# Reordering VectorE's work at stage changes, in the delta rule's output chain and in the last normalisation

## What is computed

```python
for l in range(DEPTH):                      # 2
    mod = (silu(c) @ w_ada[l] + b_ada[l])   # 9 vectors of 1024: shift, scale, gate for 3 sub-layers
    y = swiglu(x * (1 + scale) + shift, ffn_w_up[l, 0], ffn_w_down[l, 0])
    x = layer_norm(ALPHA * x + 0.5 * (1 + gate) * y, ln_g[l, 0], ln_b[l, 0])
    y = mixer(x * (1 + scale) + shift, w_in[l], ..., w_branch[l], w_o[l])
    x = layer_norm(ALPHA * x + (1 + gate) * y, ln_g[l, 1], ln_b[l, 1])
    y = swiglu(..., ffn_w_up[l, 1], ffn_w_down[l, 1])
    x = layer_norm(ALPHA * x + 0.5 * (1 + gate) * y, ln_g[l, 2], ln_b[l, 2])
```

## Time and profile before

| | |
|---|---|
| median of 3 runs | 1361.91 us (1359.81 to 1363.42) |
| the profiled execution, its own time | 1363.72 us |
| its span | 1362.0 us |
| mean granted TensorE clock | 0.98 of full speed |
| TensorE busy | 96% of the span |
| VectorE busy | 73% |
| ScalarE busy | 49% |
| GpSimd busy | 9% |
| DMA | 295.24 MB, mean 217 GB/s |

### The profile page before, as it was taken

How to read it: one execution, slowest core, us unless ns; L and a number is a source line. 1 busy time by engine, 2 the same in 40 slices (tenths; PEclk the granted TensorE clock), 3 DMA queues, 4 the chain that set the end, 5 groups by cost and what they waited for, 6 DMA issues and landing times.

```text
span 1362.0 us, 18522 instructions
## 1 busy us (share of the span) xinstructions
PE 1301.0 (96%) x7277; PEld 1077.8 (79%) x7277; DVE 996.4 (73%) x1294; ACT 664.4 (49%) x998; POOL 122.4 (9%) x219
## 2 busy tenths in 40 slices
PE   4799999999999999999999999999999999999996
PEld 3588887898888767888878888788888877788885
DVE  4778875597776787888667888559777669776545
ACT  2344444666744545445354444366675354544431
POOL 4101001000000011000100000100000001100000
PEclk9799999999899999999999999999989999999998
DMA  9679883866465447888659888467655543785550
GB/s 326 233 237 307 283 283 105 282 210 211 143 202 178 154 143 250 276 279 277 237 162 303 278 278 289 145 220 240 207 179 190 177 152 103 258 288 187 185 185 31
DMA packets 198342, 295.24 MB, mean 217 GB/s; under 512 B 14408, under 2 KB 162416, under 8 KB 198256
## 3 DMA queue, kind: packets, MB, share of 16 engines
q1 hardware_dynamic: 177744, 220.58, 48.7%
q0 software_dynamic: 20512, 73.48, 16.4%
HBM read 292.97 MB, written 1.05 MB: 216 GB/s over the span
## 4 chain that ended last, share of the span: by engine, by line
PE 78%; DVE 12%; ACT 4%; issue 3%; DMA 2%; POOL 1%; SPq 0%; DVEq 0%; POOLq 0%; ACTq 0%
PE pg L979 68%; DVE wlo L1620 3%; PE pt L1004 1%; DVE acc L1559 1%; ACT whi L567 1%; DMA wraw<-in_w_in_dram 1%; PE pt L959 1%; PE pt L1341 1%; PE pt L1328 1%; PE pt L1180 1%; DVE cv L1806 1%; PE pt L1343 1%; DVE gates L2068 1%; DVE acc L1644 1%; DVE x L1743 1%
## 5 line engine op out<-in xcount | busy, mean ns | idle before, releaser
L1620 DVE TENSOR_TENSOR wlo<-wraw,whi 128x1024 fp32r<-128x1024 f32 (+1 forms) x408 | 480.1, 1201 | 169.1 <-ACT whi L567 168.4
L567 ACT ACTIVATE whi<-wraw 128x1024 fp32r<-128x1024 f32 (+1 forms) x408 | 405.7, 1035 | 169.5 <-PE pg L979 106.1
L979 PE MATMUL pg<-whi,hhi 128*128 128x512 f32 x1024 | 417.2, 407 | 15.5 <-DVE wlo L1620 12.6
L979 PE MATMUL pg<-wlo,hhi 128*128 128x512 f32 x1024 | 405.8, 396 | 0.0
L979 PE MATMUL pg<-whi,hlo 128*128 128x512 f32 x1024 | 405.8, 396 | 0.0
L979 PEld LDWEIGHTS pg<-whi,hhi 128*128 128x128 f32 x1024 | 196.6, 192 | 62.6 <-DVE wlo L1620 16.1
L979 PEld LDWEIGHTS pg<-whi,hlo 128*128 128x128 f32 x1024 | 196.1, 192 | 42.8
L979 PEld LDWEIGHTS pg<-wlo,hhi 128*128 128x128 f32 x1024 | 196.7, 192 | 38.7 <-issue 0.5
L1644 DVE SCALAR_TENSOR_TENSOR acc<-aw,sc,acc 128x1024 f32<-128x1024 f32 x128 | 163.8, 1279 | 0.5 <-DMA aw<-in_w_ada_dram 0.4
L979 PE MATMUL pg<-whi,athi 128*128 128x512 f32 x352 | 138.4, 393 | 0.0
L444 POOL DMA_DIRECT2D aw<-in_w_ada_dram x128 | 67.9, 530 | 771.0 <-DVE acc L1644 736.3
(11 more groups left out here) (336 smaller groups left out, 1324.7 us busy)
## 6 DMA issues: line engine op xcount, KB each, us to landing
wraw<-in_ffn_w_up_dram SPq DMA_DIRECT2D x176, 512.0 KB, 5.5
aw<-in_w_ada_dram POOLq DMA_DIRECT2D x128, 512.0 KB, 4.4
wraw<-in_w_in_dram SPq DMA_DIRECT2D x104, 512.0 KB, 4.7
wraw<-in_ffn_w_down_dram SPq DMA_DIRECT2D x88, 512.0 KB, 4.7
pro<-in_w_ada_dram SPq DMA_DIRECT2D x16, 512.0 KB, 9.9
wraw<-in_w_branch_dram SPq DMA_DIRECT2D x16, 512.0 KB, 4.3
wraw<-in_w_o_dram SPq DMA_DIRECT2D x16, 512.0 KB, 3.7
lnw<-in_ln_g_dram POOLq DMA_DIRECT2D x5, 512.0 KB, 5.9
```

The costliest lines, as they stand in the source:

```text
L567: act.activation(hi_view(n)[:, 0:size], wraw[:, q, o:o + size], ACT.Copy).then_inc(S["w_hi"], 1)
L979: ins = pe.matmul(out_ap, a[i], b[j], start=first and n == 0, stop=last and n == 2, skip_group_check=group)
L1620: dve.tensor_tensor(lo, a, hi_view(n)[:, 0:size].bitcast(F32), ALU.subtract).then_inc(S["w_lo"], 1)
```

## The change

- Last normalisation: `normed` and `affine` of the last stage become `last_norm(t)`, four operations on halves of 512 columns: (x - mean) * gain for both halves, which needs no power, then * rstd + bias for both. Each half of a tile is stored by a DMA of its own (256 KB), four in all in place of two.
- Stage changes: `h_low` is called by quarter. The third quarter of tile 0 stays ahead of `residual(1, 1)`, the fourth goes behind `moments(1)`. At s = 1 VectorE's splits of the next stage's halves 2 and 3 go ahead of `residual(1, 0)` (they stood ahead of `residual(1, 1)` and behind `moments(1)`), and ScalarE makes all four splits before it modulates tile 0.
- Output chain: the multiplication behind GpSimd's power becomes `o_scale(t)`, called later than `o_mean(t)`; `o_raw` and `o_scale(0)` go ahead of `gated(1, 1)`; `o_mean(1)` and `o_gate(0)` go ahead of slot 57's split, `o_scale(1)` and `o_gate(1)` stay behind it.
- `column_parts` of the shift goes from slot 61 to slot 45; that of the scale stays at slot 64.

```diff
--- before.py
+++ after.py
@@ -376,9 +376,11 @@
             for t in range(NT):
-                sp.wait_ge(S["x_affine"], NT * (STAGES - 1) + t + 1)
-                sp.dma_start(out[0, t * P:(t + 1) * P, :], x[:, t, :]).then_inc(S["out"], 16)
-            sp.wait_ge(S["out"], 16 * NT)
+                for n in (0, 1):
+                    c = slice(n * 512, (n + 1) * 512)
+                    sp.wait_ge(S["x_affine"], NT * (STAGES - 1) + 2 * t + n + 1)
+                    sp.dma_start(out[0, t * P:(t + 1) * P, c], x[:, t, c]).then_inc(S["out"], 16)
+            sp.wait_ge(S["out"], 2 * 16 * NT)
 
@@ -624,13 +626,10 @@
                     h = 2 * u_next + (0 if s == 1 else 2)
-                    split(h)
-                    split(h + 1)
+                    for n in range(4 if s == 1 else 2):
+                        split(h + n)
                     modulate(at, s, 0, 0)
                     modulate(at, s, 0, 1)
-                    if s == 1:
-                        split(h + 2)
-                        split(h + 3)
                     modulate(at, s, 1, 0)
@@ -1600,14 +1599,13 @@
 
-            def h_low(at, k, t, half):
-
-                for quarter in (2 * half, 2 * half + 1):
-                    c = slice(2 * quarter, 2 * quarter + 2)
-                    dve.wait_ge(S["h_hi"], at("h_hi", 4 * (NT * k + t) + quarter + 1))
-                    dve.tensor_tensor(hlo[:, c, t * P:(t + 1) * P],
-                                      lnw[:, t, quarter * 256:(quarter + 1) * 256].rearrange("p (k s) -> p k s", k=2),
-                                      hhi[:, c, t * P:(t + 1) * P].bitcast(F32), ALU.subtract).then_inc(S["h_lo"], 1)
+            def h_low(at, k, t, quarter):
+
+                c = slice(2 * quarter, 2 * quarter + 2)
+                dve.wait_ge(S["h_hi"], at("h_hi", 4 * (NT * k + t) + quarter + 1))
+                dve.tensor_tensor(hlo[:, c, t * P:(t + 1) * P],
+                                  lnw[:, t, quarter * 256:(quarter + 1) * 256].rearrange("p (k s) -> p k s", k=2),
+                                  hhi[:, c, t * P:(t + 1) * P].bitcast(F32), ALU.subtract).then_inc(S["h_lo"], 1)
 
@@ -1653,9 +1651,9 @@
 
-                def shift(stage, t, rows=lnw):
+                def shift(stage, t):
                     dve.wait_ge(S["x_gain"], NT * stage + t + 1)
-                    dve.tensor_tensor(x[:, t, :], x[:, t, :], rows[:, 1, :], ALU.add).then_inc(S["x_affine"], 1)
+                    dve.tensor_tensor(x[:, t, :], x[:, t, :], lnw[:, 1, :], ALU.add).then_inc(S["x_affine"], 1)
 
@@ -1758,40 +1756,47 @@
 
-                    def affine(t):
+                    def last_norm(t):
 
                         dve.wait_ge(S["ln_rows"], 32 * STAGES)
-                        dve.wait_ge(S["ln_x"], at("ln_x", 2 * (NT * s + t) + 2))
-                        dve.tensor_tensor(x[:, t, :], x[:, t, :], last_rows[:, 0, :], ALU.mult).then_inc(S["x_gain"], 1)
-                        shift(STAGES - 1, t, last_rows)
+                        dve.wait_ge(S["ln_mv"], at("ln_mv", NT * s + t + 1))
+                        for n in (0, 1):
+                            c = slice(n * 512, (n + 1) * 512)
+                            dve.scalar_tensor_tensor(out=x[:, t, c], in0=x[:, t, c], scalar=mv[:, t, 0:1], in1=last_rows[:, 0, c],
+                                                     op0=ALU.subtract, op1=ALU.mult).then_inc(S["x_gain"], 1)
+                        dve.wait_ge(S["ln_rstd"], at("ln_rstd", NT * s + t + 1))
+                        for n in (0, 1):
+                            c = slice(n * 512, (n + 1) * 512)
+                            dve.wait_ge(S["x_gain"], NT * (STAGES - 1) + 2 * t + n + 1)
+                            dve.scalar_tensor_tensor(out=x[:, t, c], in0=x[:, t, c], scalar=rstd[:, t:t + 1], in1=last_rows[:, 1, c],
+                                                     op0=ALU.mult, op1=ALU.add).then_inc(S["x_affine"], 1)
 
...
                     moments(0)
-                    normed(0)
                     if 3 * l + s == STAGES - 1:
-                        affine(0)
+                        last_norm(0)
                         residual(1, 0)
...
                         moments(1)
-                        normed(1)
-                        affine(1)
+                        last_norm(1)
                         return
+                    normed(0)
                     h = 2 * u_next + (0 if s == 1 else 2)
-                    split(h)
-                    split(h + 1)
+                    for n in range(3 if s == 1 else 2):
+                        split(h + n)
                     h_low(at, s, 0, 0)
+                    if s == 1:
+                        split(h + 3)
+                    h_low(at, s, 0, 1)
                     residual(1, 0)
-                    h_low(at, s, 0, 1)
-                    if s == 1:
-                        split(h + 2)
+                    h_low(at, s, 0, 2)
                     residual(1, 1)
                     moments(1)
-                    if s == 1:
-                        split(h + 3)
+                    h_low(at, s, 0, 3)
                     normed(1)
-                    h_low(at, s, 1, 0)
-                    h_low(at, s, 1, 1)
+                    for quarter in range(4):
+                        h_low(at, s, 1, quarter)
 
@@ -2019,6 +2024,9 @@
                     dve.tensor_scalar(oss[:, c], oss[:, c], RMS_EPS, None, ALU.add).then_inc(S["o_ms"], 1)
+
+                def o_scale(t):
+                    c = slice(4 * t, 4 * t + 4)
                     dve.wait_ge(S["o_pw"], at("o_pw", t + 1))
@@ -2089,14 +2097,19 @@
                             gated(0, q - 49)
-                        if q in (55, 56):
-                            gated(1, q - 55)
+                        if q == 55:
+                            gated(1, 0)
                         if q == 52:
...
                             o_raw()
+                            o_scale(0)
+                            gated(1, 1)
+                        if q == 57:
+                            o_mean(1)
+                            o_gate(0)
                         if q == 59:
@@ -2139,8 +2152,7 @@
                         if q == 57:
-                            o_mean(1)
-                            o_gate(0)
+                            o_scale(1)
                             o_gate(1)
@@ -2154,8 +2166,8 @@
                             merged_lo(1)
-                        if q in (61, 64):
-                            column_parts(3 * l + 2, (61, 64).index(q))
+                        if q in (45, 64):
+                            column_parts(3 * l + 2, (45, 64).index(q))
                         if q == SLOTS - 4:
...
```

## The result

| | before | after |
|---|---|---|
| median of the runs taken side by side | 1362.66 us (4 runs) | 1349.8 us (1348.2 to 1352.61, 4 runs) |
| the profiled execution's own time | 1363.72 us | 1349.19 us |
| its span | 1362.0 us | 1347.5 us |
| mean granted clock | 0.980 | 0.984 |

The ratio is 0.9903 with a 95% interval of 0.9887 to 0.992: 12.9 us between the medians, faster by 1.0%. The forecast was 1349.6, in a range of 1343.5 to 1355.

The account below looks back on a forecast made before the run. TensorE was taken as the bound, so gains come only from its idle or half-clock moments and the end. 5.8 + 4.8 - 1.6 + 0.9 + 2.4 = 12.3 us took the median from 1361.9 to 1349.6, range 1343.5 to 1355.

Parts of the forecast that it names:

- Term 1: Output chain: TensorE's waits for gated output products go in both layers, with one half-clock stretch; gain 5.8 us.
- Term 2: Shift columns at slot 45: the sum fits VectorE's wait for ScalarE, merged_lo(0) comes earlier; gain 4.8 us.
- Term 3: Mixer to feed-forward: ScalarE stands for a weight unit's DMA before modulating tile 0, x comes later; loss 1.6 us.
- Term 4: Other three stage changes: one h_low quarter leaves VectorE's queue ahead of residual(1, 1); gain 0.9 us.
- Term 5: The end: halved last normalisation runs partly beside GpSimd's power, and smaller stores land sooner; gain 2.4 us.
- A: Mixer to feed-forward: the weight unit is there in time, ScalarE isn't held; 1344 to 1345 us, chance 0.12.
- B: Idle pieces at mixer to feed-forward bring half clock, or output chain keeps part of its wait; 1353 to 1354, chance 0.18.
- C: TensorE is limited elsewhere in the mixer and takes back output-chain and shift-column gains; 1358 to 1361 us, chance 0.07.
- D: Slower: each us the weight unit lands late moves x by a us in both layers; 1366 and more, chance 0.03.

Follow-up runs that it names:

- The undivided operation: Changed kernel with the gain operation of the last normalisation over a tile's 1024 columns at once in place of two halves; 1348.6 us, single run.
- the two experiments on the splits: Changed kernel with the mixer to feed-forward splits put back on both engines, 1346.46 us; with only VectorE's put back, ScalarE's new order kept, 1352.56 us.
- the four that were run in repeat: Changed kernel with one edit put back each: output chain 1357.59 us, shift columns 1353.2, last normalisation 1351.82, splits at mixer to feed-forward 1346.46.

## Why the prediction was right

The mechanisms of four terms came out as forecast and that of the fifth in part. That the median hit 1349.8 for 1349.6 is luck beyond that. By the landmarks the change's own work is -6.6 (output chain), -4.8, +1.4, -0.7 and -2.8, together 13.5 us; forecast were 12.3, and the medians gave 12.9. The forecast was also taken from a median of 1361.91, and the one beside the changed kernel was 1362.66. Each of these is smaller than the 4 us over which the runs of one kernel scatter.

- **Term 1, output chain: 6.6 for 5.8.** The last product was forecast for 459.0; the timeline after runs 1.0 us earlier there (slot 55's split starts at 449.10 for 450.10), and it ended at 457.95. The mis-sized part is "some 0.1 of restarting": with the waits of 1.57 and 1.84 gone, the stretch up to the transposes is 1.7 and 2.0 shorter, and behind them 0.7 instead of 0.4. The half-clock stretch, 1.4 forecast, was worth 1.6. That stretch isn't the second layer's own, as the prediction counted it: the undone chain had it in both, so its share is the luck of the profiled execution.
- **Term 2, shift columns: 4.78 for 4.8.** The step from VectorE's queue to TensorE's waits held in both directions, and so did the cover: the 2.4 us fit into the 3.23 and left 0.83. The new wait of 0.3 forecast at the last half didn't come.
- **Term 3, mixer to feed-forward: a loss of 1.37 for 1.6.** This is the step that the runs had to decide, since VectorE's queue alone promises a gain. With the landing moved from 502.4 to 496.5 and 5.8 us subtracted, residual(1, 1) was forecast for 504.1 and started at 503.95, x for 507.4 and came at 507.31. One line of the working is wrong as written: 4.15 less the split's 1.2 plus 0.12 is 3.1, not 3.3. What goes is the 0.92 by which the split lengthened the power, not its 1.2 (VectorE waited for the power anyway), and that gives the 3.3 that was used; 3.36 was measured. Both waits of TensorE came, 0.7 and 2.2 us for 1 and 2.3. ScalarE's order alone costs 2.6 to 2.9 us, VectorE's new order gives back 2.0 to 2.2.
- **Term 4, other stage changes: 0.66 for 0.9.** The quarter adds 0.11 us to GpSimd's power, not 0.07 (term 3 had put it at 0.12), and a quarter is 0.33 in a queue, not 0.37.
- **Term 5, the end: 2.83 for 2.4.** Here a step was wrong in kind. I let the power be held by both operations that run beside it (1.1 us longer, 1.65 in all). It took 1.02: GpSimd got in between the two, and VectorE didn't wait. The undivided operation gives 1.58, close to what I had taken. From residual(1, 1) to VectorE's end it took 5.2 us for 6.8 before, 1.6 instead of 1.1 gained; the 0.63 ahead of it (0.64 forecast) and the 0.62 of the store (0.65 forecast) came as worked out.
  The Trainium skill (SBUF — State Buffer, SBUF: two separate sides) states that of a VectorE instruction with two SBUF inputs and a GpSimd instruction that reads SBUF, the one that starts first holds the shared ports for its whole length and the other is blocked. The 1.58 us row agrees for one instruction, and the 1.02 us row shows the lock given up at the end of the first of two. I had let the second VectorE instruction take it again ahead of GpSimd, and that was the wrong part.
- **Rivals.** A falls with the two experiments on the splits. B's clock part is real as a scatter: between x(1) and the next gate rows it takes 160.3 us, or 161.6 with half clock, and over the executions each layer showed both; that is 1.3 us per layer where B counted 2 to 3. C falls with the single edits. They add up by the landmarks; by the medians, undoing the four that were run in repeat gives 7.8 + 3.4 + 2.0 - 3.3 = 9.9 us of 12.9, where the fourth quarter's share is missing and each number carries a scatter of 1 to 2 us. D's mechanism exists (the unit that came 0.8 us late), at a size far from deciding.

## What to carry to other kernels

When a step is moved ahead on an engine that works in order, look up when its input lands, not only what its own queue gains: here a split pulled forward in its queue stood for a DMA and held a tile's whole modulation behind it, while the same split placed behind three quarters of the modulation, 0.3 us after the landing, stood for nothing and made the fastest version. A reduction whose result is needed late belongs into the largest idle time of its engine after its inputs are complete. Landmarks on the bound engine's timeline resolve a tenth of a microsecond where three to five runs resolve two.

## What the runs showed of the hardware

- Half clock came and went with identical code. The stretch from the sums of squares to the output transposes, without a wait at its end, takes 110.22 or 111.84 us in these executions, and with the old wait 113.6 to 115.5: steps of 1.6 us, in either layer. Granted clock of two stretches of the changed kernel with the same instructions, behind x(1) in the first and the second layer (busy time with counts by engine, granted clock, DMA share, GB/s):

```profile
509.00:512.50 3.50, 3.50 (x11) 2.74 (x10) 1.11 (x3) 3.40 (x11) 0.00 (x0) 0.54 0.00 0
1156.90:1160.40 3.50, 3.47 (x15) 2.53 (x15) 1.15 (x3) 3.40 (x11) 0.00 (x0) 1.00 0.00 0
```

  Both follow a wait of 2.2 us, and one is at 1.2 GHz and the other at 2.4. What decides between them stays open; no run was made for it.
- GpSimd's power of 128 values took 0.55 us alone, 0.67 beside one VectorE operation of 0.41 with two SBUF inputs, 1.02 beside two of 0.75, 1.47 beside one of 1.22 and 1.58 beside one of 1.28: it waits for the operation that has started, and no longer. In all four cases it took 0.55 us and the started operation's duration less 0.25 to 0.3.
- The four stores of 256 KB landed 2.0 to 2.1 us after issue, the two of 512 KB took 2.6.
